# Two attention stages: stacks built one head at a time, and TensorE's order within a unit

## The reference

```python
def forgetting_attention(q, k, v, c):
    scale = 1.0 / math.sqrt(HEAD_DIM)
    for s in range(0, T, BLOCK_Q):
        e = s + BLOCK_Q
        logits = jnp.einsum('bhqd,bhkd->bhqk', q[:, :, s:e], k[:, :, :e]).astype(jnp.float32) * scale
        logits = logits + (c[:, :, s:e, None] - c[:, :, None, :e])
        causal = jnp.arange(s, e)[:, None] >= jnp.arange(e)[None, :]
        logits = jnp.where(causal, logits, -jnp.inf)
        p = jax.nn.softmax(logits, axis=-1).astype(v.dtype)
        outs.append(jnp.einsum('bhqk,bhkd->bhqd', p, v[:, :, :e]))
```

## Time and profile before

| | |
|---|---|
| median of 3 runs | 2735.14 us (2729.79 to 2739.59) |
| the profiled execution | 2729.75 us, its span 2727.7 us |
| mean granted TensorE clock | 0.942 |
| TensorE matmul (PE) busy | 2506.9 us, 92% |
| TensorE weight load (PEld) | 1996.9 us, 73% |
| VectorE (DVE) busy | 1314.2 us, 48% |
| GpSimd (POOL) busy | 1290.8 us, 47% |
| ScalarE (ACT) busy | 540.5 us, 20% |
| chain that ended last | PE 80%, DVE 12%, ACT 3%, issue 3%, POOL 2% |

### The profile page before, as it was taken

The page is one execution under the profiler, slowest core; times in us unless marked ns, Lnnn a source line. Parts: engine busy times, 40 slices in busy tenths (PEclk is TensorE's granted clock), DMA queues, the critical chain, the costliest instruction groups (busy, mean ns, idle before and its releaser), DMA issues.

```text
span 2727.7 us, 42157 instructions
## 1 busy us (share of the span) xinstructions
PE 2506.9 (92%) x17122; PEld 1996.9 (73%) x17122; DVE 1314.2 (48%) x1631; ACT 540.5 (20%) x1093; POOL 1290.8 (47%) x824
## 2 busy tenths in 40 slices
PE   4998999989999999966699999999999688999999
PEld 2783799958888877634578888788788366788887
DVE  8597655566424352235564333517212566743333
ACT  6533100022101020114421010200100553211100
POOL 1564000026666655423356666666664123566665
PEclk9998899899999999977799999999999678999999
DMA  2220000023333332210023333333332000233332
GB/s 98 78 85 0 3 3 3 3 86 93 99 95 99 93 93 87 68 42 1 1 77 94 100 93 100 93 93 95 123 100 70 19 1 16 85 93 99 93 100 85
DMA packets 50032, 188.10 MB, mean 69 GB/s; under 512 B 5568, under 2 KB 5696, under 8 KB 49376
## 3 DMA queue, kind: packets, MB, share of 16 engines
q1 hardware_dynamic: 49392, 182.32, 21.6%
q10 hardware_dynamic: 496, 3.64, 0.4%
HBM read 183.77 MB, written 2.10 MB: 68 GB/s over the span
## 4 chain that ended last, share of the span: by engine, by line
PE 80%; DVE 12%; ACT 3%; issue 3%; POOL 2%; DMA 0%; DVEq 0%; POOLq 0%; ACTq 0%
PE ps L501 21%; PE ps L502 20%; PE ps L503 20%; PE ps L900 2%; PE ps L665 1%; PE ps L526 1%; PE ps L915 1%; PE ps L678 1%; PE ps L513 1%; PE ps L673 1%; PE ps L881 1%; DVE ssq L1405 1%; PE ps L596 1%; PE ps L882 1%; PE ps L639 1%
## 5 line engine op out<-in xcount | busy, mean ns | idle before, releaser
L397 POOL TENSOR_SCALAR whi<-raw 128x1024 fp32r<-128x1024 f32 x334 | 358.8, 1074 | 1110.0 <-PE ps L503 785.5
L400 POOL TENSOR_TENSOR wlo<-raw,whi 128x1024 fp32r<-128x1024 f32 x334 | 817.2, 2447 | 27.8
L501 PE MATMUL ps<-HH,whi 128*128 128x512 f32 x1056 | 417.2, 395 | 7.8 <-DVE HL L1555 5.1
L502 PE MATMUL ps<-HL,whi 128*128 128x512 f32 x1056 | 413.0, 391 | 0.0
L503 PE MATMUL ps<-HH,wlo 128*128 128x512 f32 x1056 | 412.7, 391 | 0.0
L501 PE MATMUL ps<-hidH,whi 128*128 128x512 f32 x768 | 298.8, 389 | 0.0
L502 PE MATMUL ps<-hidL,whi 128*128 128x512 f32 x768 | 298.8, 389 | 0.0
L503 PE MATMUL ps<-hidH,wlo 128*128 128x512 f32 x768 | 298.8, 389 | 0.0
L1602 DVE TENSOR_TENSOR X<-X,ps 128x512 f32<-128x512 f32 x192 | 123.3, 683 | 306.4 <-PE ps L503 306.4
L501 PEld LDWEIGHTS ps<-HH,whi 128*128 128x128 f32 x1056 | 199.1, 189 | 64.3 <-issue 14.7
L503 PEld LDWEIGHTS ps<-HH,wlo 128*128 128x128 f32 x1056 | 199.5, 189 | 41.9
(11 more groups left out here) (399 smaller groups left out, 4069.0 us busy)
## 6 DMA issues: line engine op xcount, KB each, us to landing
raw<-stream SPq DMA_DIRECT2D x334, 512.0 KB, 3.6
X<-xT SPq DMA_DIRECT2D x2, 1024.0 KB, 6.1
X<-xT SPq DMA_DIRECT2D x1, 2048.0 KB, 7.9
CW<-cmpw ACTq DMA_DIRECT2D x1, 2048.0 KB, 8.0
out<-X SPq DMA_DIRECT2D x4, 512.0 KB, 2.6
cst<-consts SPq DMA_DIRECT2D x1, 735.5 KB, 8.3
c2f<-consts ACTq DMA_DIRECT2D x1, 722.0 KB, 4.7
c2s<-consts ACTq DMA_DIRECT2D x1, 722.0 KB, 4.1
```

What stands on the lines that cost most here:

```text
L397: pool.tensor_scalar(whi[:, s, :, :], raw[:, j, :].rearrange("p (k m) -> p k m", k=DT), 1.0, 0.0, ALU.mult, ALU.add)\
L400: pool.tensor_tensor(wlo[:, s, :, :], raw[:, j, :].rearrange("p (k m) -> p k m", k=DT), whi[:, s, :, :].bitcast(F32), ALU.subtract)\
L501: pe.matmul(acc, whi[:, s, k, :], hi, start=start, stop=False)
L502: pe.matmul(acc, whi[:, s, k, :], lo, start=False, stop=False)
```

## The change

The diff changes three streams. GpSimd: the first three head stacks are built ahead of unit 0; then the second head of pair p+1 follows the normalisation of the first unit of pair p, and the first head of pair p+2 that of its last unit. Where it had waited for its own copies at the end of a stack, it now waits ahead of each normalisation. TensorE: scores(u+2) stand behind turn(u) and no longer ahead of values(u-1). VectorE: one head's subtractions follow transposed(u) for v = 0 and one head's for v = 1; before, both heads' stood ahead of the maxima at v = per_pair - 2. ACT's stream is unchanged.

```diff
--- before.py
+++ after.py
@@ -426,23 +426,21 @@
 
                 per_pair = len([x for x in units if x[1] == 0])
 
-                def stacks(p):
-
-                    if p:
-                        pool.wait_ge(*count(f"{tag}_pnp", (p - 1) * per_pair + 1))
+                def stack(p, hp, normalised):
+
+                    if p == 0 and hp == 0:
+                        pool.wait_ge(S("split_ready"), last_split)
+                    elif p < 2 and normalised == 0:
+                        pool.wait_ge(*count(f"{tag}_q_nat", 2 * p + hp))
                     else:
-                        pool.wait_ge(S("split_ready"), last_split)
-                    if p >= 2:
+                        pool.wait_ge(*count(f"{tag}_pnp", normalised))
+                    if p >= 2 and hp == 0:
                         pool.wait_ge(*count(f"{tag}_s", (p - 1) * per_pair))
-                    for hp in range(2):
-                        h = data(hp)
-                        if hp:
-                            pool.wait_ge(*count(f"{tag}_q_nat", 2 * p + 1))
-                        if keys is not None:
-                            pool.tensor_scalar(KSA[h, p % 2, hp, :], keys(p)[h, :], 1.0, 0.0, ALU.mult, ALU.add).then_inc(S("fa_k_hi"), 1)
-                            pool.tensor_scalar(KSB[h, p % 2, hp, :], keys(p)[h, :], 1.0, 0.0, ALU.mult, ALU.add).then_inc(S("fa_k_b"), 1)
-                        pool.tensor_scalar(B["QA"][h, p % 2, hp, :], src(p)[h, :], 1.0, 0.0, ALU.mult, ALU.add).then_inc(count(f"{tag}_q_nat", 0)[0], 1)
-                    pool.wait_ge(*count(f"{tag}_q_nat", 2 * p + 2))
+                    h = data(hp)
+                    if keys is not None:
+                        pool.tensor_scalar(KSA[h, p % 2, hp, :], keys(p)[h, :], 1.0, 0.0, ALU.mult, ALU.add).then_inc(S("fa_k_hi"), 1)
+                        pool.tensor_scalar(KSB[h, p % 2, hp, :], keys(p)[h, :], 1.0, 0.0, ALU.mult, ALU.add).then_inc(S("fa_k_b"), 1)
+                    pool.tensor_scalar(B["QA"][h, p % 2, hp, :], src(p)[h, :], 1.0, 0.0, ALU.mult, ALU.add).then_inc(count(f"{tag}_q_nat", 0)[0], 1)
 
                 def normalise(u):
                     name, p, i = units[u]
@@ -452,13 +450,17 @@
                     pool.tensor_scalar(probs, probs, B["col"][:, u % 4, 2, 1:2], 1.0 if gate is None else gate(name, p, 1, i),
                                        ALU.mult, ALU.mult).then_inc(count(f"{tag}_pnp", 0)[0], 1)
 
+                pairs = len(units) // per_pair
+                for p, hp in ((0, 0), (0, 1), (1, 0)):
+                    stack(p, hp, 0)
                 for u in range(len(units)):
                     p, v = divmod(u, per_pair)
-                    if u == 0:
-                        stacks(0)
+                    pool.wait_ge(*count(f"{tag}_q_nat", min(2 * p + (4 if v else 3), 2 * pairs)))
                     normalise(u)
-                    if v == 0 and p + 1 < len(units) // per_pair:
-                        stacks(p + 1)
+                    if v == 0 and p + 1 < pairs:
+                        stack(p + 1, 1, u + 1)
+                    if v == per_pair - 1 and p + 2 < pairs:
+                        stack(p + 2, 0, u + 1)
 
             pool.wait_ge(*count("qn2_used", DT))
             pool.wait_ge(*count("kn2_used", DT))
@@ -919,11 +921,11 @@
                 scores(0)
                 scores(1)
                 for u in range(len(units)):
-                    if u + 2 < len(units):
-                        scores(u + 2)
                     if u:
                         values(u - 1)
                     turn(u)
+                    if u + 2 < len(units):
+                        scores(u + 2)
                 values(len(units) - 1)
 
             def fox_pair(p):
@@ -1693,9 +1695,9 @@
                 def keys(u):
                     return CMPB if units[u][0] == "cmp" else P * (units[u][2] + 1)
 
-                def queries(p):
-
-                    for hp in range(2):
+                def queries(p, heads=(0, 1)):
+
+                    for hp in heads:
                         h = data(hp)
                         if fox_keys is not None:
                             dve.wait_ge(*count("fa_k_hi", 2 * p + hp + 1))
@@ -1745,10 +1747,10 @@
                     p, v = divmod(u, per_pair)
                     normalise(u)
                     if u + 2 < len(units):
-                        if v == per_pair - 2:
-                            queries(p + 1)
                         maxima(u + 2)
                     transposed(u)
+                    if v < 2 and p + 1 < pairs:
+                        queries(p + 1, (v,))
                     if v == 1 and p:
                         output(p - 1)
                 output(pairs - 1)
```

## The result

The changed kernel took 2855.28 us (median of 4 runs, 2849.52 to 2859.54), the one before 2734.01 (median of 4): a ratio of 1.0441, with a 95% interval of 1.0412 to 1.0469. It is 121 us slower; the forecast was 2856.

What follows compares the result with a forecast made beforehand. TensorE bounds the kernel nearly everywhere (92% busy), except the two attention stretches. Loop and clock there give +123 us, slow dense work 2: 2729.75 + 125 = 2855, given as 2856, range 2775 to 2885.

Steps and rivals of the forecast that it cites:

- The gaps go: TensorE's attention waits for the next stack (41.6 us; 9.3 in the second stretch) and GpSimd's normalisation (11.7) go.
- rival C: Attention stretches: gaps pay in full and later scores find cover; 55 us faster, 2680; chance 0.05.
- The loop: Each attention unit: normalise, transposes, scores, maxima, copy cannot overlap; +39 us at full clock, +138 at half.
- The clock: TensorE in both attention stretches: half clock taken for 85%, 39 + 0.85 x 99 = 123 us.
- the low end: TensorE holds full clock in the attention stretches, by the skill's rule on long gaps: +39 us.
- Subtractions cost 3.0 and 1.4 us a pair, uncovered: VectorE's stack subtractions, where they now stand, are covered by no wait: 3.0 us a pair, 1.4 in the second stretch.
- Removed gaps "just pay for the loop if the clock is full": First attention stretch at full clock: 142.2 us between first and last reciprocal, 138.2 before, so +4.0.
- The start behind the stretches: Dense work behind the attention stretches starts slow: 2 us.
- B: Attention stretches: the loop, with the clock mostly full; 2774 us, up to 2815; chance 0.26.
- D: The change's two parts cancel within 0.3% (8 us), chance 0.03, or slow it by less than B, chance 0.04.

Runs made afterwards that it cites:

- experiment 1: The change with TensorE's order put back to the old one, so stacks one head at a time alone: 2690.86 us, ratio 0.9838.
- (2): TensorE's new order alone, with the stacks of the kernel before the change: 2842.02 us, ratio 1.0394.
- (3): The change, with VectorE copying the transposes of u before it takes the maxima of u+2: 2784.12 us, ratio 1.0177.
- (4): The change, with TensorE's order values of u-1, scores of u+2, transposes of u: 2780.25 us, ratio 1.0163.
- experiment 7: The change, with 14 gapless matmuls of 512 columns on TensorE ahead of each attention stretch: 2875.79 us, ratio 1.0528.
- experiment 6: The change, with VectorE's subtractions for the next stack moved ahead of the maxima: 2813.40 us, ratio 1.0287.
- 11: TensorE's old order, GpSimd's copies one head at a time, VectorE's subtractions where they were before the change: 2738.97 us, ratio 0.9995.
- Experiment 5: The change, with 8 matmuls of 128 columns between values(u-1) and the transposes in each unit after the first: 2883.32 us, ratio 1.0542.

## Why the prediction was right, step by step

**The gaps go.** Right: 41.6 to 7.2 us, and 9.3 in the second stretch to none but the start. The sum has no term for them, since it adds up the new loop whole; rival C had them at 55 us. In the old order they were worth 44 (experiment 1), and there the wait for the stack only fell to 23.4 us: in the change it is the slower units that cover the rest.

**The loop.** Right, and it carries the result. Four kernels say it: the old order on TensorE removes the loss (1), TensorE's order alone brings it (2), and the loop is shortened from VectorE's end (3) and from TensorE's (4), each by over 70 us. Its terms held too: in the first stretch the maxima took 26.4 us (26.3 in the working), the copies 15.4 (15.7), the subtractions 19.2 (21.1), GpSimd's normalisations 20.8 (21.9). At the granted clock of 0.61, 78% of the first stretch is at half clock, so the working gives 142.2 + 0.78 x 47.1 = 178.9, for 176.9 measured; at 0.56 it gives 172.0 + 0.88 x 52.5 = 218.2, for 212.6.

**The clock.** The share of half clock, 85%, was a choice between two ends 99 us apart, and came out 78% and 88%. What I based it on, that the loop never offers a gapless stretch, is not quite what the trace shows. Windows of TensorE in the change:

```profile
1249.20:1252.60 3.40, 3.40 (x24) 0.50 0.00 0
1252.60:1256.00 3.40, 1.93 (x22) 0.91 0.00 0
1256.00:1259.40 3.40, 1.66 (x12) 1.00 0.01 2
1259.40:1262.80 3.40, 2.43 (x8) 0.59 0.00 0
```

The values of 384 keys, the transposes of 512 and the scores of 256 do make a gapless piece (here from 1248.8 to 1253.4, and again from 1296.2 to 1300.9), and the clock rises behind it; in the last of these rows, with idle time in the two before, it is at 0.59 again. The rule of the Trainium skill (TensorE: Matmul & The Clock Gate, section HAM oscillation — how this bites in real kernels), that long gaps between bursts are what returns the clock to half, gave the low end. Experiment 1 agrees with it: the gaps are shorter, few new waits took their place, and the clock is 0.83 for 0.73. The change does not: the gaps of 5 us are gone and the clock is lower than before, 0.60 for 0.73, and in experiment 7 it fell behind a first wait of 1.3 us. Many short waits did what the few long ones had done.

**Subtractions cost 3.0 and 1.4 us a pair, uncovered.** Right in the new order for the first stretch, where taking them out of the loop gave 38 us, more than their 21; in the second it gave nothing (experiment 6). The prediction might have said more plainly that they then make a loss of the first part of the change. In the old order the same move belongs to a gain (experiments 1 and 11).

**Removed gaps "just pay for the loop if the clock is full".** Experiment 5 is in line with it for the first stretch (143 us left when the fill is taken off by estimate, at 0.92). No run had full clock without added work, so it is not shown.

**The start behind the stretches.** I gave 2 us for dense work that begins at half clock. Between the last reciprocal of the first stretch and the first of the second lie 791.3 us before, 798.1 in the change, 791.5 in experiment 1: some 7. In the first 10.9 us behind the last reciprocal TensorE is at 0.50, where it was at 1.00 before. The last values and transposes take 8.0 us there for 5.5, which no term of the sum held; the dense work behind them is at half clock for its first 3.3 us, which costs some 1.7, so the 2 was about right. The other 2.6 are not explained; kernels with the old order scatter from 791.3 to 794.7 between these points.

**Rivals.** B and C fell: B by experiment 7, C since the wait of the maxima in the first stretch grew from 15.9 to 100.0 us, 2.6 a unit, and not under 0.7. D did not come into play.

**The number.** That 2856 came within 1 us of 2855.28 is luck in good part. The sum has 123 us for the two stretches, which grew by 113.9; the 7.0 ahead of them are in no term, and the 6.8 between them stand against 2. The errors go opposite ways.

## What to carry to other kernels

In hand-ordered engine streams a step that is moved on one engine must be followed into the order of every engine that consumes it: here scores went behind the transposes on TensorE, while VectorE still took the maxima of those scores ahead of copying the transposes, and two independent chains became one loop through 80 units. Before such a move, write down one unit's path around all engines and ask what can still run beside what. And try the parts of a change apart: this one held a gain of 44 us under a loss of 165, and the better kernel of the study is simply the change without its second part, 2691 us against 2735 before on the same chip.

## What was not expected of the hardware

TensorE's clock reacts to idle time in short pieces. In the changed kernel no wait of TensorE inside the stretches, behind the first one of each, was longer than 1.9 us, and by what they waited for they were 0.8 to 1.4 us in the mean; there were one or two of them in a unit of 4.5 to 5.7 us, and the clock was at half for most of both stretches (PEclk 0.61 and 0.56). Added matmuls ahead of the transposes raised it to 0.79 and 0.81 (three per unit) and to 0.92 and 0.95 (eight), with the wait for the copy left as it was. The time did not follow: three were 13 us below the change, 5 of them in the stretches, and eight 28 us above it. A start at full clock did not last beyond the first units. In the old order, with the same transposes, scores and values, the clock was 0.83 and 0.82.
